# Gate matrix of the expert mixer: indirect accumulating DMAs into a cleared array in place of one-hot products

## What is computed

```python
s1 = einsum('thd,hnd->thn', q[:, :, 0], k1); s2 = einsum('thd,hnd->thn', q[:, :, 1], k2)
v1, i1 = top_k(s1, 16); v2, i2 = top_k(s2, 16)
sv, si = top_k(v1[..., :, None] + v2[..., None, :], 16)     # of 256 candidates
eidx = (i1 * 128 + i2)[si]; gates = softmax(sv)
act = gelu(einsum('phkd,pd->phk', u_tab[eidx], x))
out = einsum('phk,phkd->pd', gates * act, v_tab[eidx])
```

## Time and profile before

| | |
|---|---|
| median of 3 runs | 4672.34 us |
| the profiled execution | 4669.94 us, span 4668.2 us |
| `experts_in_stage`, first to last block product | layer 0: 1001.0 to 1897 us, layer 1: 3017 to 3905 us |
| `delta_stage` | about 339 to 683 us |
| busy over the span | PE 92%, DVE 69%, ACT 38%, POOL 31% |

### The profile page before, as it was taken

The page is one execution under the profiler, slowest core; times in us unless marked ns, Lnnn a source line. Parts: engine busy times, 40 slices in busy tenths (PEclk is TensorE's granted clock), DMA queues, the critical chain, the costliest instruction groups (busy, mean ns, idle before and its releaser), DMA issues. The chain is left out here.

```text
span 4668.2 us, 58501 instructions
## 1 busy us (share of the span) xinstructions
PE 4298.8 (92%) x21997; PEld 3603.2 (77%) x21997; DVE 3216.9 (69%) x5003; ACT 1785.2 (38%) x3370; POOL 1436.3 (31%) x844
## 2 busy tenths in 40 slices
PE   6988888899999999899999877999999997999997
PEld 1988886687888877688888476888888776888885
DVE  3658863338779876688888623187897865888886
ACT  1330002223667666222222232235777663222222
POOL 1001100100112123566777301000121234777763
PEclk9999988999999999999999988999999998999998
DMA  5210002344587788988888502455787889888884
GB/s 206 69 37 5 1 37 72 144 160 153 193 257 238 228 278 279 327 287 293 289 292 287 208 29 85 149 170 166 239 251 233 266 289 310 295 291 287 294 287 168
DMA packets 566628, 951.23 MB, mean 204 GB/s; under 512 B 295264, under 2 KB 317024, under 8 KB 560992
## 3 DMA queue, kind: packets, MB, share of 16 engines
q1 hardware_dynamic: 188000, 534.59, 33.5%
q0 software_dynamic: 73728, 268.47, 16.0%
q10 hardware_dynamic: 304640, 144.73, 10.6%
HBM read 794.56 MB, written 153.09 MB: 203 GB/s over the span
## 5 line engine op out<-in xcount | busy, mean ns | idle before, releaser
L757 POOL DMA_INDIRECT p1uring<-in_urows,p1eidx x128 | 171.7, 1342 | 851.0 <-DVE p1ew L872 608.2
L757 POOL DMA_INDIRECT p0uring<-in_urows,p0eidx x128 | 166.5, 1300 | 862.6 <-DVE p0ew L872 621.3
L624 PE MATMUL p0ups<-hi,p0uwhi 128*128 128x512 f32 x1024 | 419.0, 409 | 12.4 <-DVE p0uwlo L767 12.4
L624 PE MATMUL p1ups<-hi,p1uwhi 128*128 128x512 f32 x1024 | 417.0, 407 | 11.3 <-DVE p1uwlo L767 11.3
L986 PE MATMUL p1vps<-p1vwhi,p1vvhi 128*128 128x512 f32 x1024 | 399.2, 390 | 23.6 <-DVE p1vwlo L950 23.6
L986 PE MATMUL p0vps<-p0vwhi,p0vvhi 128*128 128x512 f32 x1024 | 399.4, 390 | 20.3 <-DVE p0vwlo L950 20.3
L624 PE MATMUL p0ups<-lo,p0uwhi 128*128 128x512 f32 x1024 | 404.8, 395 | 0.0
L624 PE MATMUL p0ups<-hi,p0uwlo 128*128 128x512 f32 x1024 | 404.4, 395 | 0.0
L624 PE MATMUL p1ups<-lo,p1uwhi 128*128 128x512 f32 x1024 | 402.9, 393 | 0.0
L624 PE MATMUL p1ups<-hi,p1uwlo 128*128 128x512 f32 x1024 | 402.6, 393 | 0.0
L986 PE MATMUL p0vps<-p0vwhi,p0vvlo 128*128 128x512 f32 x1024 | 399.1, 390 | 0.0
(11 more groups left out here) (464 smaller groups left out, 10928.6 us busy)
## 6 DMA issues: line engine op xcount, KB each, us to landing
p0uraw<-in_u SPq DMA_DIRECT2D x128, 512.0 KB, 4.2
p0vraw<-in_vrows SPq DMA_DIRECT2D x128, 512.0 KB, 3.9
p1uraw<-in_u SPq DMA_DIRECT2D x128, 512.0 KB, 4.2
p1vraw<-in_vrows SPq DMA_DIRECT2D x128, 512.0 KB, 3.8
slab<-in_ada_w SPq DMA_DIRECT2D x24, 2048.0 KB, 7.6
a_scratch<-p0ua_out ACTq DMA_DIRECT2D x128, 256.0 KB, 4.0
g_scratch<-p0ug ACTq DMA_DIRECT2D x32, 1024.0 KB, 9.6
p0vga<-g_scratch SPq DMA_DIRECT2D x128, 256.0 KB, 4.1
```

Of the source, the lines that this page charges most:

```text
L624: mm = nc.tensor.matmul(psums[b % 2][:], x[:, b % 3, c * P:(c + 1) * P], y[:, c, S_CTX:T], start=c == 0 and n == 0, stop=c == NC - 1 and n ...
L757: nc.gpsimd.indirect_dma_start(out=ring[:, n % RING, :], out_offset=None, in_=table, in_offset=bass.IndirectOffsetOnAxis(ap=eidx[:, n:n + ...
```

## The change

The sample tiles are routed first, all five tiles in the same rhythm: scores at blocks 1, 15, 29, 43 and 57, and 12 blocks for the 21 tasks; the prompt tile is the last. All of the quads, one-hots, gate products, turned copies, the buffer g and its stores are gone. Instead DVE works out, for each sample tile, the flat cell of every gate in the array [first key][second key][token] (`gidx`) and the gate (`gval`), and POOL adds them into that array: 128 indirect DMAs per tile, each of 128 single values (one per token, 4 bytes each) with an add. The 16 DMAs of one head name different experts; those of the next head of the same tile wait until all of them have landed, so POOL takes two tiles in turn, head by head (`phase_plan`). The gathers of the prompt tile, now into a ring of 6, stand in the same POOL order behind them: the first two heads' gathers come after head 4 of the last sample tile, 464 of the 512 accumulating DMAs being issued before. The dots are spread over blocks 74 to 125. Both layers' arrays are separate, and both are cleared in `delta_stage` by 32 stores of 2 MB.

```diff
+SCATTERED = DEC_TILES
+ORDER = (*range(1, TILES), 0)
+SCORES = [1 + 14 * r for r in range(TILES)]
+DOT0 = 74
-RING = 3
+RING = 6
 def route_plan(n_tasks):
+    for r, s in enumerate(SCORES):
+        for i in range(n_tasks):
+            plan[s + 2 + i * 12 // n_tasks].append((r, i))
 def dot_plan():
+    for n in range(PAIRS):
+        plan[DOT0 + n * (P - 2 - DOT0) // PAIRS].append(n)
+def phase_plan():
+    H = PEER_HEADS // 2
+    plan = [(0, h) for h in range(H)]
+    for t in range(SCATTERED - 1):
+        for h in range(H):
+            plan += [(t, H + h), (t + 1, h)]
+    for h in range(H):
+        plan += [(SCATTERED - 1, H + h), (SCATTERED, 2 * h), (SCATTERED, 2 * h + 1)]
     return plan
...
         @block.gpsimd
         def _(pool):
+            cells = g_dram.rearrange("i p t -> (i p t)").rearrange("(n o) -> n o", o=1)
+            for t, h in phase_plan():
+                if t < SCATTERED:
+                    if h == 0:
+                        pool.wait_ge(scat_ready, 2 * (t + 1))
+                    else:
+                        pool.wait_ge(scattered[t], 16 * TOPK * h)
+                elif h == 0:
+                    pool.wait_ge(listed, 1)
+                for n in range(h * TOPK, (h + 1) * TOPK):
+                    if t < SCATTERED:
+                        nc.gpsimd.indirect_dma_start(out=cells, out_offset=bass.IndirectOffsetOnAxis(ap=gidx[:, t, n:n + 1], axis=0),
+                                                     in_=gval[:, t, n:n + 1], in_offset=None, compute_op=ALU.add).then_inc(scattered[t], 16)
+                    else:
+                        if n >= RING:
+                            pool.wait_ge(dot_done, n - RING + 1)
+                        nc.gpsimd.indirect_dma_start(out=ring[:, n % RING, :], out_offset=None, in_=table,
+                                                     in_offset=bass.IndirectOffsetOnAxis(ap=eidx[:, n:n + 1], axis=0)).then_inc(row_full[n % RING], 16)
+            for sem in scattered:
+                pool.wait_ge(sem, 16 * PAIRS)
...
             def gates(k):
+                if k < SCATTERED:
+                    st.link(v.scalar_tensor_tensor(out=flat_idx[:], in0=rows[:, 0, :], scalar=float(P), in1=rows[:, 1, :],
+                                                   op0=ALU.mult, op1=ALU.add))
+                    v.scalar_tensor_tensor(out=gidx[:, k, :], in0=flat_idx[:], scalar=float(S_DEC), in1=tokens[:, k, :],
+                                           op0=ALU.mult, op1=ALU.add).then_inc(scat_ready, 1)
...
             split_lo(0)
             split_lo(1)
+            v.tensor_tensor_reduce(flat_idx[:], ident, iota, 1.0, 0.0, ALU.mult, ALU.add, pcol[:]).then_inc(pcol_ready, 1)
+            for t in range(SCATTERED):
+                st.done(v.tensor_scalar(tokens[:, t, :], m["ones"][:], pcol[:, 0:1], float(t * P), ALU.mult, ALU.add))
...
 def delta_stage(...):
+    CLEAR = 8
+        zeros = sb("zeros", [P, CLEAR, SCATTERED * P])
             sp.dma_start(states[1][:], d["state"]).then_inc(full, 16)
+            sp.wait_ge(blank, 1)
+            for dst in g_dram:
+                for i in range(0, P, CLEAR):
+                    sp.dma_start(dst[i:i + CLEAR, :, 0:SCATTERED * P].rearrange("i p t -> p i t"), zeros[:]).then_inc(cleared, 16)
             sp.wait_ge(s_new, DH)
...
             sp.wait_ge(st_out, 16)
+            sp.wait_ge(cleared, 16 * DEPTH * P // CLEAR)
...
             widen(units[0][0])
+            v.memset(zeros[:], 0.0).then_inc(blank, 1)
```

More of the change, by code:

```diff
@@ L472, in add_to_x @@
     return evacuate
-QUAD = 4
-NQ = P // QUAD
 DEC_TILES = S_DEC // P
[L478 to L485, removed]
-PAIRS = P
-RING = 3
[L490 to L496, removed]
+SCATTERED = DEC_TILES
+ORDER = (*range(1, TILES), 0)
+SCORES = [1 + 14 * r for r in range(TILES)]
+DOT0 = 74
+PAIRS = P
+RING = 6
 def route_plan(n_tasks):
     plan = [[] for _ in range(P)]
-    for k, s in enumerate(SCORES):
-        span = (12, 11)[k] if k < 2 else WIN - 6
+    for r, s in enumerate(SCORES):
         for i in range(n_tasks):
-            plan[s + 2 + i * span // n_tasks].append((k, i))
+            plan[s + 2 + i * 12 // n_tasks].append((r, i))
     return plan
 def dot_plan():
[L511 to L516, removed]
+    plan = [[] for _ in range(P)]
+    for n in range(PAIRS):
+        plan[DOT0 + n * (P - 2 - DOT0) // PAIRS].append(n)
+    return plan
+def phase_plan():
[6 more added lines that the diff above has]
+        plan += [(SCATTERED - 1, H + h), (SCATTERED, 2 * h), (SCATTERED, 2 * h + 1)]
     return plan
@@ L524, in experts_in_stage @@
     hi_done, lo_done, mm_done, act_done = (sm(x) for x in ("hi_done", "lo_done", "mm_done", "act_done"))
[L525 to L529, removed]
+    spilled, keys_full, q_full, scored, s_taken, exp_ready, exp_done, ready = (
+        sm(x) for x in ("spilled", "keys_full", "q_full", "scored", "s_taken", "exp_ready", "exp_done", "ready"))
+    steps, cand_used = (
+        sm(x) for x in ("steps", "cand_used"))
     h_turned, h_taken, listed, dot_done, gelu_done, weighed = (
         sm(x) for x in ("h_turned", "h_taken", "listed", "dot_done", "gelu_done", "weighed"))
+    pcol_ready, paired, scat_ready = sm("pcol_ready"), sm("paired"), sm("scat_ready")
+    scattered = [sm(f"scattered{t}") for t in range(SCATTERED)]
     table = d[f"urows{l}"]
@@ L595, in _ @@
                         load_q(k)
-                    if b == SCORES[k] - (0 if k < 3 else 3):
+                    if b == SCORES[k]:
                         load_keys(k)
@@ L604, in _ @@
             mm.then_inc(h_turned, 1)
[L606 to L613, removed]
             for b in range(P):
-                todo = list(quads[b])
                 pe.wait_ge(lo_done, b + 1)
@@ L638, in _ @@
                         mm.then_inc(scored, 1)
[L639 to L643, removed]
         @block.scalar
@@ L651, in split_hi @@
                 nc.scalar.copy(whi[:, b % 3, :], raw[:, b % 2, :]).then_inc(hi_done, 1)
[L653 to L687, removed]
             def finish(b):
@@ L725, in _ @@
                     nc.scalar.activation(ex[:], ex[:], ACT.Exp).then_inc(exp_done, 1)
[L726 to L744, removed]
             act.wait_ge(dot_done, PAIRS)
@@ L767, in split_lo @@
                 v.tensor_tensor(wlo[:, b % 3, :], raw[:, b % 2, :], whi[:, b % 3, :].bitcast(F32), ALU.subtract).then_inc(lo_done, 1)
[L769 to L773, removed]
-                    if n >= 3:
-                        dve.wait_ge(made, n - 2)
-                    rows_of = ((oh2, 0, near), (oh1, 1, one1)) if n % 2 else ((oh1, 1, one1),)
-                    for oh, row, sem in rows_of:
-                        v.tensor_tensor(oh[:, n % 3], iota.unsqueeze(1).to_broadcast([P, QUAD, P]),
-                                        tops[:, k % 2, row, t0:t0 + QUAD].unsqueeze(2).to_broadcast([P, QUAD, P]), ALU.is_equal).then_inc(sem, 1)
             def top16(source, h0, out_v, out_i):
@@ L829, in gates @@
                 st.link(v.reciprocal(rden[:], den[:]))
-                out = gate[:] if k else eg[:].rearrange("p (h k) -> p h k", h=PEER_HEADS)
-                v.tensor_tensor(out, ex[:], rden[:].unsqueeze(2).to_broadcast([P, PEER_HEADS, TOPK]), ALU.mult).then_inc(ready, 1)
-                if k == 0:
+                by_head = lambda x: x.rearrange("p (h k) -> p h k", h=PEER_HEADS)
+                out = by_head(eg[:]) if k == SCATTERED else by_head(gval[:, k, :])
+                product = v.tensor_tensor(out, ex[:], rden[:].unsqueeze(2).to_broadcast([P, PEER_HEADS, TOPK]), ALU.mult)
+                product.then_inc(*((scat_ready, 1) if k < SCATTERED else (ready, 1)))
+                if k == SCATTERED:
                     v.scalar_tensor_tensor(out=eidx[:], in0=rows[:, 0, :], scalar=float(P), in1=rows[:, 1, :],
                                            op0=ALU.mult, op1=ALU.add).then_inc(listed, 1)
+                if k < SCATTERED:
[3 more added lines that the diff above has]
+                                           op0=ALU.mult, op1=ALU.add).then_inc(scat_ready, 1)
+                    dve.sem_inc(ready, 1)
             def route(k, i):
@@ L838, in route @@
                     dve.wait_ge(s_taken, 4 * (k + 1))
-                    if k > 1:
-                        dve.wait_ge(turned, k - 1)
+                    if 1 <= k <= SCATTERED:
+                        dve.wait_ge(scat_ready, 2 * k)
                 if i < 8:
@@ L1511, in tokens_stage, with delta_stage @@
     sm.close()
-def delta_stage(nc, m, d, qkv, tok, lg, beta, gcol, o_acc, state_out, hh, acc, cw, taps_before):
+def delta_stage(nc, m, d, qkv, tok, lg, beta, gcol, o_acc, state_out, hh, acc, cw, taps_before, g_dram):
     sm = Sems(nc, "delta")
@@ L1869, in build @@
         q_dram = nc.dram_tensor("q_scratch", [NSC, P, T], F32, kind="Internal").ap()
-        g_dram = nc.dram_tensor("g_scratch", [P, P, S_DEC], F32, kind="Internal").ap()
```

(3 more changed lines are left out.)

44 lines of the change are left out of this document (13 added, 31 removed).

## The result

The changed kernel takes 5611.9 us (median of 4, 5607.1 to 5618.84) against 4671.87 (median of 4): a ratio of 1.2013, 95% interval 1.1992 to 1.2033, 940 us slower. The forecast was 5030, slower by 358. The profiled execution is 5607.1 us, span 5605.3.

A forecast was written before the change was run, and what follows sets the result against it. PE, busy 92% of the span, was taken to bound the kernel; POOL's adds ahead of the gathers would lengthen both in-stages: 4669.9 + 356 + 3.5 (memset), about 5030 us, range 4500 to 5700.

The forecast's parts named there:

- The mechanism: In both in-stages DVE stands once near block 74 for a gather's row, 200 to 300 us, PE waiting behind on `split_lo`.
- The step that failed: POOL's price per accumulating DMA, taken from a gather: 1.62 us while DVE routes, 1.24 us while DVE stands still.
- The upper bound: POOL's accumulating DMA at the blocked 1.68 + 0.30 = 1.98 us in every case, or more if DMA engines limit it.
- The contention term: Gathers on POOL stand until a two-input DVE operation ends: 1.62 us a DMA with such meetings, 1.24 us back to back.
- After it: Behind the first row: PE's 51 blocks 278 us, POOL's 176 DMAs 285 us; the larger ends the stage at 1070 us.
- the floor of 788 us: `experts_in_stage` if the first row arrives before PE stands: 488 + 54 x 5.45 + 6 = 788 us.
- Rival 1: DMA engines become the bound on the adds, 2.6 us a DMA; kernel about 6100 us; chance 0.15.
- Rival 2: Adds cheap on POOL, under 0.83 us: stage 788 us, kernel 4466 us; break-even at 1.06 us; chance 0.22.
- Rival 3: Every add on POOL blocked by DVE's two-input work, pitch 1.98 us throughout; kernel about 5670 us; chance 0.08.
- the forecast's own range of 4800 to 5150: Kernel time around the 5030 us forecast, which keeps chance 0.50; the range with rivals is 4500 to 5700.
- Rival 4: Clearing stores in `delta_stage` aren't hidden and add up to 270 us to the forecast, 5300 us; chance 0.05.
- PE's clock: After the stand before block 77, a few blocks at the lower clock level, at most a few us per layer; taken as 0.

## Why the prediction was right on the sign and wrong on the size

- **The mechanism held.** One stand of DVE per layer for a gather's row, PE behind it on `split_lo`, POOL busy nearly without a gap from the first tile's gates on (1100.1 - 1005.6 = 94.5 us into the stage; 95.5 worked out).
- **The step that failed** is "I take the gather's price, the nearest row: 1.62 us while DVE routes, 1.24 us while DVE stands still". Measured: 222.06 / 121 + 0.30 = 2.13 us while DVE routes and 472.42 / 306 + 0.30 = 1.84 us in the stand. Both are dearer by 0.5 to 0.6 us, and the stores without an add show that this is the add's own price. The prediction put it at nothing because no row showed an accumulating DMA. The upper bound stood at 1.98 us with the gap, taken from a gather that meets a DVE operation. But the two costs come on top of one another: an add that meets nothing holds POOL for 1.55 us, and while DVE routes, meetings bring the mean to 222.06 / 121 = 1.84 us, without the gap. The contention term itself, +0.29 us a DMA, was put at +0.38.
- **The same sum with the measured prices.** DVE stands from 446 us into the stage (dot 0 was put at 488). Heads 0 to 4 of the first tile end at 94.5 + 80 x 2.13 + 16 = 281 us; (446 - 281) / 2.13 = 77 adds follow until then, and the other 307 at 1.84 take 565. That puts the first gather at 1011 us; it went at 2019.6 - 1005.6 = 1014. Predicted were 777: the price of the adds in front is 237 of the 295 us by which each layer came out longer (1365 against 1070).
- **After it** 351 us passed where 293 were worked out. POOL's gathers cost what they did before: the window from 2020 on holds 252.37 us, of which the adds take 844.3 - 68.3 - 222.1 - 472.4 = 81.5, so 171 / 128 = 1.34 us a gather as in the earlier trace rows. The 48 adds between them take 2.0 us each with the gap in place of 1.62 (+18 us), and POOL waited 40 us for dots to free the ring, a wait that the prediction left out. The sum for the adds uses this group of the page, part 5:

```profile
L680 POOL DMA_INDIRECT g_scratch<-p0ugval,p0ugidx x512 | 844.3, 1649 | 404.3 <-DVE p0ugidx L758 232.8
```

- **A misreading of the earlier trace rows.** Block 15 and block 30, not 29, have their `split_lo` at the two times shown: 16 of these have begun by 1088.3 us and 31 by 1180.7. So 15 blocks took 92.4 us, 6.16 us a block and not 6.6, and dot 0 should have stood at 456 us. In the sum this takes 7 us off (770 in place of 777); in the floor of 788 us for a stage that no row delays it takes 32 off (756), and without adds that stage took 736. A smaller one: the 163 us in the earlier trace rows are POOL's time for 125 gathers, not for a layer's 128; the 1.31 us each is right.

```profile
L767 DVE TENSOR_TENSOR p0uwlo<-p0uraw,p0uwhi x16: 1203/1224/1227, 999.7 to 1088.3; 128x1024 fp32r<-128x1024 f32 x16
```

```profile
L767 DVE TENSOR_TENSOR p0uwlo<-p0uraw,p0uwhi x31: 1203/1224/1227, 999.7 to 1180.7; 128x1024 fp32r<-128x1024 f32 x31
```

- **Rival 1** (DMA engines) fell: adds land in 3.0 us, POOL waits 16 us at the heads (18 were put down), and in the stand the engines are busy to 0.23. **Rival 2** (cheap adds) fell by the price; its break-even pitch of 1.06 us lies under even a plain store's (0.958 + 0.30). **Rival 3** gives 5670, near the result, but its mechanism is not what happened: in the stand DVE is idle and an add still takes 1.55 us. That 5611.9 lies within 4500 to 5700 is luck for the same reason; the forecast's own range of 4800 to 5150 missed it. **Rival 4** fell: clearing is hidden.
- **PE's clock** was granted at 0.50 in the first 6 us in which blocks run again (2028 to 2034 us) and at 1.00 from 2040 to 2060 us: a few us at most, as taken. Behind the stand POOL's gathers set the pace in any case (PE busy 282 of 345 us).

## What to carry to other kernels

An operation that the trace doesn't show may belong to another class than its nearest row: leave the upper bound room for its own price and for contention together, since here they added up. Work moved from a bound engine to an idle one has to be summed against that engine's whole queue, and the last consumer in that queue (here the gathers behind 464 adds) is who pays. Before moving all of such work, move as much as the idle engine has room for: a quarter of the adds gained 1.2% where all of them lost 20%.

## What the runs showed of the hardware

An accumulating indirect DMA of 128 values of 4 bytes holds POOL for 1.55 us; a plain store or fetch of the same cells 0.95 us, and a gather of 128 rows of 4 KB about as much (0.93 to 1.00). The add also splits the transfer, into 144 packets per DMA in queue 0 against 32, but a gather has 144 too and costs POOL 0.94 us. So the 0.59 us come with the add and not with the number of packets; what POOL does in that time stays open.

Meetings with DVE lengthen an add as they do a gather, and not every DVE operation counts. POOL and DVE beside one another:

```profile
1178.05 3.16 POOL L680 DMA_INDIRECT g_scratch<-p0ugval,p0ugidx  x1 [0.30 <-issue]
1181.51 1.55 POOL L680 DMA_INDIRECT g_scratch<-p0ugval,p0ugidx  x1 [0.30 <-issue]
```

```profile
1177.50 2.29 DVE L738 TENSOR_TENSOR xT<-xT,p0uidxf 128x2048 f32<-128x2048 f32 x1
1179.82 2.29 DVE L742 TENSOR_REDUCE p0urows<-xT 128x128 f32<-128x2048 f32 x1
```

The first add began while DVE ran a product of two SBUF tensors and ended 1.42 us after it; the second began beside a sum over one tensor and took its plain 1.55 us. Of layer 0's 512 adds 61 were lengthened, 59 of which began beside an operation with two SBUF inputs (`split_lo`, dots, some steps of the routing); three more began in the last 0.02 us of one and were not. Of the 85 that began beside any other DVE operation none was. The Trainium skill (SBUF — State Buffer, the box "DVE blocks DMA") tells of POOL being kept from writing descriptors while DVE runs an operation in a 2-port perf mode. What the rows here show goes by two SBUF inputs, and as single meetings, not as a standing state.
